# An encoder layer: modulation, projections, convolution and states as one stage over pairs of tiles, in three-term fp32r products

## The chip, the cores and the metric

The kernel runs on one core of a Trainium2 chip (trn2). The metric is the device time of one launch in microseconds. A core has five engines that the text names: TensorE (PE; PEld are its weight loads), VectorE (DVE), ScalarE (ACT), GpSimd (POOL) and SyncE (SP), which here only issues DMAs. Each engine works through its own queue in order and waits on semaphores that others raise.

## What is computed

One encoder layer for two requests, a prompt of 512 tokens and a sample of 1024, both 1024 wide: twelve tiles of 128 tokens, tiles 0 to 3 the prompt's, 4 to 11 the sample's. Cut to what matters here:

```python
mod = silu(c) @ w_ada + b_ada                       # (6 * 1024) per request
sh1, sc1, g1, sh2, sc2, g2 = split(mod)
h = rmsnorm(x, norm1_w) * (1 + sc1) + sh1
proj = h @ w_in                                     # 1024 x 1696
cq, ckv, kr, z, xbc, dt_raw = split(proj)           # 256, 128, 32, 512, 768, 16
y_attn = mla(cq, ckv, kr, ...)                      # 8 heads, over the whole request
xbc = silu(dwconv(xbc, conv_w, 5 taps, centred) + conv_b)
dt = softplus(dt_raw + dt_bias)
# states of each chunk of 128 tokens, forward and backward:
states = einsum(bm, exp(cs[-1] - cs) * dt, x);  carry = carry * exp(cs[-1]) + states
y_ssd = rms((y_fwd + y_bwd + d_skip * x) * silu(z)) * ssd_norm_w
x = x + g1 * (concat(y_attn, y_ssd) @ w_out)
h = rmsnorm(x, norm2_w) * (1 + sc2) + sh2
y = rmsnorm(x + g2 * expert_choice_moe(h))          # 16 experts
```

All inputs and outputs are fp32.

## The kernel before

The kernel is a list of stages, each a block in which the engines have queues of their own, with a barrier between blocks: `modulation`, `projections`, `convolution`, `states`, `attend` (for the prompt and then the sample `keys` and `mixers`), `output`, `choice`, `experts`, `final`. The order of work in a queue is the order in which it is written.

`modulation` takes the first four of twelve slabs of w_ada (512 columns, 2 MB each), through a ring of four buffers: 64 instructions of TensorE a slab with silu(c) as the stationary side (`mod_rows`, L262), a copy by VectorE, one turn into columns (`mod_columns`, L271). SyncE also starts the loads of the first two tiles and of w_in.

`projections` goes over tiles, with the work of the next tile ahead (`tile_pipeline`). ScalarE sums the squares (L407), VectorE scales (L440), TensorE turns eight blocks (L483), both take them with shift and gain (L416, L447), and TensorE multiplies in fp32: latents (L496, 416 columns), z (L500), steps (L514, 16 columns) and xbc by channels, 6 blocks of 128 channels x 128 tokens (L520). An fp32 product is two instructions. Tiles 2 to 9 take one late slab each, between z and the steps (L262 again, and L478 for the turn). All results of all tiles stay in SBUF.

`convolution`: softplus and decays for all tiles at once on VectorE, ScalarE and TensorE, the first tap on ScalarE (L574), the other four on VectorE (L620), 512 or 1024 tokens an instruction. `states` goes over tiles one at a time: silu (L699), turns and B/C products (L753 to L758), weighing of x for both directions (L733), state products (L766), and then `scan` on VectorE over all tiles in both directions (L785, L792). SyncE stores what the mixers need to DRAM, one record of 1920 values a tile.

`mixers` goes over tiles: eight heads of attention, with the SSD products between them. A tile's record and query latents are loaded one or two tiles ahead. The steps `dta`, `dt` and the decays are read from SBUF, where the convolution left them; `terms` on VectorE (L1234) and on POOL (L1061) make the sums' operands out of them.

The experts, which are not changed, already split weights and rows in a high and a low fp32r part and multiply in three terms (L2098 and L2099 for gate and up, L2109 for down).

## Time and profile before

| | us |
|---|---|
| median of 3 runs | 3337.61 |
| lowest, highest | 3326.56, 3339.79 |
| the profiled execution: its time | 3328.14 |
| its span, first to last instruction | 3326.5 |
| modulation, to | 37 |
| projections, to | 378 |
| convolution, to | 431 |
| states, to | 518 |
| keys and mixers of both requests, to | 1162 |

The busy time of an engine is a share of a stage and says nothing by itself of what bounds it: an engine that is never idle bounds; where none is, the waits between them do. The granted clock is a mean of TensorE's two levels, 1.2 and 2.4 GHz, over a stretch: 1.00 is all at 2.4, 0.5 all at 1.2.

### The profile page before, as it was taken

What the parts mean: (1) busy time and instruction counts of PE and PEld (TensorE: products, weight loads), DVE (VectorE), ACT (ScalarE), POOL (GpSimd) and SP (SyncE); (2) the same over time, 40 slices, a digit from 0 to 9 for tenths busy, and PEclk for the clock granted to TensorE, in tenths of its full rate; (3) what the DMA queues carried; (4) which work ended last, traced back from release to release, by engine and by line L of the source; (5) the groups of instructions that cost most, each with busy time, mean ns of one, the idle gap of its engine ahead of it and who ended that gap; (6) DMA issues with size and microseconds to landing.
All of it is one profiled execution on the core that took longest, in us unless ns stands there. A gap on an engine that the chain in (4) does not pass through costs nothing. (4 is left out here: it accounts for less than half of the span.)

```text
span 3326.5 us, 51133 instructions
## 1 busy us (share of the span) xinstructions
PE 2939.6 (88%) x17924; PEld 2396.3 (72%) x17924; DVE 2105.9 (63%) x3908; ACT 1479.8 (44%) x2832; POOL 177.7 (5%) x180
## 2 busy tenths in 40 slices
PE   6999544868999789639999999999999999999993
PEld 4777422544666545339999999999999999999993
DVE  1111474655666523487887788778877887788774
ACT  1111232454445412125555555555555555555553
POOL 0000000101110000000000000000000000000001
PEclk8999766988999989769999999999999999999996
DMA  6121022001011043257777777677767776777764
GB/s 244 64 95 69 19 105 84 31 20 43 21 40 38 21 152 126 76 170 229 247 246 224 238 248 243 225 243 245 240 225 246 246 238 217 254 248 225 231 212 161
DMA packets 355693, 544.53 MB, mean 164 GB/s; under 512 B 11280, under 2 KB 283920, under 8 KB 355600
## 3 DMA queue, kind: packets, MB, share of 16 engines
q1 hardware_dynamic: 346704, 511.83, 45.9%
q0 software_dynamic: 8896, 31.46, 4.0%
q8 instruction: 58, 0.95, 0.1%
q14 instruction: 35, 0.29, 0.0%
HBM read 492.13 MB, written 51.12 MB: 163 GB/s over the span
## 5 line engine op out<-in xcount | busy, mean ns | idle before, releaser
L2098 PE MATMUL banks<-rowsT_parts,weights_high 128*128 128x384 f32 x4096 | 1184.7, 361 | 12.4 <-DVE hidden_parts L2029 7.5
L2099 PE MATMUL banks<-rowsT_parts,weights_low 128*128 128x192 f32 x4096 | 1026.6, 251 | 0.0
L2098 PEld LDWEIGHTS banks<-rowsT_parts,weights_high 128*128 128x128 f32 x4096 | 770.5, 188 | 21.6 <-DVE hidden_parts L2029 9.9
L2099 PEld LDWEIGHTS banks<-rowsT_parts,weights_low 128*128 128x128 f32 x4096 | 783.7, 191 | 1.4
L2109 PE MATMUL banks<-weights_high,hidden_parts 128*128 128x512 f32 x1536 | 435.4, 392 | 0.0
L2016 DVE TENSOR_TENSOR gate_up_sums<-banks,gate_up_sums 128x192 f32<-128x192 f32 x512 | 181.1, 354 | 329.3 <-ACT gate_up_sums L1934 329.3
L1934 ACT ACTIVATE gate_up_sums<-banks 128x192 f32<-128x192 f32 x512 | 164.9, 322 | 453.3 <-PE banks L2099 449.4
L2109 PEld LDWEIGHTS banks<-weights_high,hidden_parts 128*128 128x128 f32 x1536 | 283.4, 188 | 69.9
L2109 PE MATMUL banks<-weights_low,hidden_parts 128*128 128x512 f32 (+1 forms) x1024 | 319.6, 393 | 0.0
L1966 DVE TENSOR_TENSOR weights_low<-slab_up,weights_high 128x1024 fp32r<-128x1024 f32 x256 | 311.6, 1217 | 0.0
L1966 DVE TENSOR_TENSOR weights_low<-slab_down,weights_high 128x1024 fp32r<-128x1024 f32 x256 | 311.2, 1216 | 0.0
L1966 DVE TENSOR_TENSOR weights_low<-slab_gate,weights_high 128x1024 fp32r<-128x1024 f32 x256 | 311.0, 1215 | 0.0
L1908 ACT ACTIVATE weights_high<-slab_up 128x1024 fp32r<-128x1024 f32 x256 | 269.1, 1051 | 0.2 <-DMA slab_up<-w_up 0.2
L1908 ACT ACTIVATE weights_high<-slab_down 128x1024 fp32r<-128x1024 f32 x256 | 264.2, 1051 | 8.5 <-PE banks L2109 7.0
L1908 ACT ACTIVATE weights_high<-slab_gate 128x1024 fp32r<-128x1024 f32 x256 | 267.9, 1047 | 0.0
L2109 PEld LDWEIGHTS banks<-weights_low,hidden_parts 128*128 128x128 f32 (+1 forms) x1024 | 164.9, 161 | 55.6
L1942 ACT ACTIVATE silu_gate<-gate_up_sums 128x192 f32<-128x192 f32 x256 | 92.5, 361 | 226.3 <-DVE gate_up_sums L2016 226.3
L1683 PE MATMUL banks<-arena_modulation 128*128 128x512 f32 x384 | 172.1, 603 | 10.5 <-DMA arena_modulation<-mixed 10.5
L1384 PE MATMUL banks<-arena_modulation 96*128 96x512 f32 x320 | 161.6, 621 | 1.6 <-DVE arena_modulation L1220 1.6
L1225 DVE TENSOR_REDUCE mix_top<-banks 128x1 f32<-128x1024 f32 (+1 forms) x96 | 100.1, 1042 | 75.3 <-PE banks L1384 74.6
L1683 PEld LDWEIGHTS banks<-arena_modulation 128*128 128x128 f32 x384 | 72.3, 193 | 93.7 <-issue 93.7
L1881 POOL DMA_INDIRECT residual<-weighted,rows_out x32 | 49.8, 1557 | 1678.1 <-DVE weighted L2005 1678.1
(263 smaller groups left out, 3389.9 us busy)
## 6 DMA issues: line engine op xcount, KB each, us to landing
slab_gate<-w_gate SPq DMA_DIRECT2D x128, 1024.0 KB, 5.5
slab_up<-w_up SPq DMA_DIRECT2D x128, 1024.0 KB, 7.4
slab_down<-w_down SPq DMA_DIRECT2D x128, 1024.0 KB, 4.9
arena_modulation<-w_ada SPq DMA_DIRECT2D x12, 2048.0 KB, 8.4
arena_modulation<-ssd_tiles SPq DMA_DIRECT2D x12, 960.0 KB, 5.1
arena_modulation<-x_sample SPq DMA_DIRECT2D x16, 512.0 KB, 6.5
mixed<-arena_modulation SPq DMA_DIRECT2D x12, 512.0 KB, 2.8
arena_modulation<-mixed SPq DMA_DIRECT2D x12, 512.0 KB, 5.5
```

The costliest lines, as they stand in the source:

```text
L1225: nc.vector.tensor_reduce(top[:, h % 2:h % 2 + 1], core.banks[:, h % 2 * 1024:h % 2 * 1024 + keys_n], AX_X, ALU.max).then_inc(topped, 1)
L1384: mm = nc.tensor.matmul(core.banks[:, h % 2 * 1024 + k0:h % 2 * 1024 + k0 + 512], qT[j][0:DQK, h, :], kT[0:DQK, h, k0:k0 + 512], start=Tru ...
L1683: mm = nc.tensor.matmul(core.ps[6 * j + half], mt[j][:, k, :], wo[:, k, 512 * half:512 * half + 512], start=(k == 0), stop=(k == 7))
L1881: nc.gpsimd.indirect_dma_start(core.residual, bass.IndirectOffsetOnAxis(ap=rows_out[b][:, 0:1], axis=0), y[b][:], None, compute_op=ALU.add ...
L1908: nc.scalar.activation(like(n, w_hi), unit_of(raw, n), ACT.Copy).then_inc(unit_hi, 1)
L1934: nc.scalar.activation(sums[:, kind, fc % 2], core.ps[2 * (fc % 2) + kind][:, CT:2 * CT], ACT.Copy).then_inc(low_out, 1)
L1942: nc.scalar.activation(sil[:, fc % 2], sums[:, 0, fc % 2], ACT.Silu).then_inc(sil_done, 1)
L1966: nc.vector.tensor_tensor(like(n, w_lo), unit_of(raw, n), like(n, w_hi[:].bitcast(F32)), ALU.subtract).then_inc(unit_lo, 1)
L2016: nc.vector.tensor_tensor(sums[:, kind, fc % 2], core.ps[2 * (fc % 2) + kind][:, 0:CT], sums[:, kind, fc % 2], ALU.add).then_inc(sum_done, 1)
L2098: nc.tensor.matmul(out[:, 0:2 * CT], w_hi[:, u, block], x[:, k, :], start=k == 0, stop=False)
L2099: mm = nc.tensor.matmul(out[:, 0:CT], w_lo[:, u, block], x[:, k, 0:CT], start=False, stop=k == KD - 1)
L2109: mm = nc.tensor.matmul(y_banks[b][0:rows, cols], h_parts[:, fc, tokens], w[:, u, cols], start=step == 0 and first, stop=step == STEPS - 1 ...
```

## The change

`inputs` takes the place of the first four stages. It works on pairs of tiles (`NPAIR` is 6), and its code is written out for all pairs; nothing of it loops.

- Slabs 0 to 3 go through a ring of two buffers. w_in comes in seven pieces, which ScalarE copies to an fp32r high part and VectorE subtracts to a low part; the steps' 16 columns now stand behind the latents', so that one product has 432 columns. The modulated input is split in the same way (`high`, `shift`), from one full-precision buffer (`full`), and turned through one PSUM bank in two halves.
- Each product is three: high x high, high x low, low x high (`terms`). xbc is made for two tiles at once: 256 columns, 6 x 8 x 3 products a pair. Latents and z stay by tile, 24 products each.
- Convolution, softplus, decays, silu, turns, chunk products and states of the pair before run in the same queues, on 256 tokens an instruction. The forward scan keeps one carry (`scan`), the backward one runs at the end of each request (`back`).
- Results go to DRAM by tile: latents (`nat_out`), z (now after silu), steps and decays, x, B/C products, states; the buffers of latents, z and x are single ones.
- `keys` loads latents of all tiles from DRAM before it begins. The mixers read steps and decays from the tile's record, now 1984 values, so `terms` wait for that record.
- The eight late slabs move to the sample's mixers, one a tile, at its last head.

The core of the diff; new functions are cut to what sets the order.

```diff
+            def terms(out, pairs):
+                for k in range(KD):
+                    for n, (a, b) in enumerate(pairs(k)):
+                        mm = nc.tensor.matmul(out, a, b, start=(k == 0 and n == 0), stop=(k == KD - 1 and n == 2))
+                return mm
...
+            def channels(p):
+                for c in range(KC):
+                    xbc(p, c)
+                    if c < 4:
+                        turn(2 * p + 2 + c // 2, c % 2)
+                    if c == 0:
+                        chunk_state(2 * p - 3)
+                    if c == 4:
+                        decays(p - 1)
...
+            for p in range(1, NPAIR):          # TensorE
+                a = 2 * p
+                channels(p)
+                nat(a)
+                zed(a)
+                nat(a + 1)
+                chunk(a - 2)
+                zed(a + 1)
+                chunk(a - 1)
+                chunk_state(a - 2)
...
+            def take_x(t):                     # ScalarE
+                if has(t):
+                    act.wait_ge(xt_mm, t + 1)
+                    if t:
+                        act.wait_ge(xw_done, 2 * t)
+                        act.wait_ge(xn_out, 16 * t)
+                    nc.scalar.activation(xnat, b_S1, ACT.Copy).then_inc(xnat_done, 1)
...
+            for p in range(NPAIR + 1):         # VectorE
+                a, q = 2 * p, p - 1
+                normalise(a + 2)
+                scan(a - 4)
+                weigh(a - 3)
+                soft1(q)
+                if p < NPAIR:
+                    take_xbc(p, 0)
+                soft2(q)
+                shift(a + 2)
+                normalise(a + 3)
+                scan(a - 3)
+                if p < NPAIR:
+                    take_xbc(p, 1)
+                soft3(q)
+                shift(a + 3)
...
+                state_weights(q)
+                if q < NPAIR - 1:
+                    convolve(q)
...
@@ mixers, VectorE
-            def terms(g):
-
+            def terms(g, j):
+
+                dve.wait_ge(tile_in[j], turn_of(g, j) + 16)
                 dve.wait_ge(seg_mm, g * 4)
...
@@ mixers, TensorE
                     if h == 7:
+                        if r:
+                            pe.wait_ge(o_mixed, g)
+                            if before:
+                                late_turn(i - 1)
+                            late_products(i)
                         turn_y(g)
...
-STAGES = [modulation, projections, convolution, states, attend, output, choice, experts, final]
+STAGES = [inputs, attend, output, choice, experts, final]
```

ScalarE's turn of a pair is: table load, `stats` of two tiles, `first_tap`, `soft_exp`, `shift`, `soft_log`, `high`, `shift`, `high`, `decays`, `take_nat`, `take_z`, `silu` of two tiles, `take_nat`, `take_x`, `take_z`, `take_x`.

How the change moves work on VectorE: before, the last rows of the convolution, which stand behind all projections and ahead of all states (L620 the taps, 512 or 1024 tokens each; L626 and L627 the state weights).

```order
L620 SCALAR_TENSOR_TENSOR arena_modulation<-arena_modulation,cols 128x512
L618 REGISTER_ALU
L620 ISA
L620 SCALAR_TENSOR_TENSOR arena_modulation<-arena_modulation,cols 128x1024
L611 REGISTER_ALU
L611 COMPARE_AND_BRANCH
L626 TENSOR_TENSOR arena_modulation<-arena_modulation 128x12x8
L627 TENSOR_TENSOR arena_modulation<-arena_modulation 128x12x8
L632 COPY chunk_decay<-arena_modulation 64x96 x2
```

After, VectorE's rows at the end of pair 5, without tile inputs to shift (L641 the channels of the bank, L648 to L653 the halo, L715 the taps of one pair, L743 the weighing of x):

```order
L641 COPY arena_inputs<-banks 128x2x256
L648 COPY arena_inputs<-arena_inputs 128x6x2
L649 COPY arena_inputs<-arena_inputs 128x6x2
L653 MEMSET arena_inputs 128x6x2
L696 TENSOR_TENSOR arena_inputs<-arena_inputs 128x2x8
L697 TENSOR_TENSOR arena_inputs<-arena_inputs 128x2x8
L700 COPY chunk_decay<-arena_inputs 64x16 x2
L715 SCALAR_TENSOR_TENSOR arena_inputs<-arena_inputs,cols 128x256 x24
```

The taps of a pair now stand between the copies of the next pair's channels and the chunk work, in the queue in which the shifts of the inputs stand too.

SyncE's queue at a middle pair after the change (L378 steps and decays, L369 latents, L373 z, L384 C, L389 x, L391 B/C products). Before, it held in the projections only loads of tiles and slabs.

```order
L378 DMA ssd_tiles<-arena_inputs 128x64
L369 DMA latents<-arena_inputs 128x416
L373 DMA ssd_tiles<-arena_inputs 128x512
L384 DMA ssd_tiles<-arena_inputs 128x128
L378 DMA ssd_tiles<-arena_inputs 128x64
L369 DMA latents<-arena_inputs 128x416
L373 DMA ssd_tiles<-arena_inputs 128x512
L384 DMA ssd_tiles<-arena_inputs 128x128
L389 DMA ssd_tiles<-arena_inputs 128x512
L391 DMA ssd_tiles<-arena_inputs 128x256
L389 DMA ssd_tiles<-arena_inputs 128x512
L391 DMA ssd_tiles<-arena_inputs 128x256
```

The store of x of the tile two back (the first L389) stands behind the stores of z and C of the pair's second tile.

TensorE at the end of a middle tile of the sample's mixers, before (L1397 turns of the probabilities, L1466 the turn of y):

```order
L1384 MATMUL banks<-arena_modulation 128x512 x2
L1393 REGISTER_ALU
L1397 MATMUL banks<-masks,arena_modulation 128x128 x8
L1466 MATMUL banks<-masks,arena_modulation 128x128 x4
L994 REGISTER_ALU
```

and after (L1646 and L1728 are the same two):

```order
L1633 MATMUL banks<-arena_attend 128x512 x2
L1642 REGISTER_ALU
L1646 MATMUL banks<-masks,arena_attend 128x128 x8
L1712 MATMUL banks<-masks,arena_attend 128x128
L1703 ISA
L1706 MATMUL banks<-arena_attend,silu_c_cols 2x128 x32
L1728 MATMUL banks<-masks,arena_attend 128x128 x4
```

One turn and 32 products (64 instructions of the profile) stand ahead of the turn of y.

## Rows read from the trace of the kernel before

**Rows 1.** The page: span; two groups of the experts (busy, mean ns | idle).

```profile
span 3326.5 us, 51133 instructions
...
L2098 PEld LDWEIGHTS banks<-rowsT_parts,weights_high 128*128 128x128 f32 x4096 | 770.5, 188 | 21.6 <-DVE hidden_parts L2029 9.9
...
L1966 DVE TENSOR_TENSOR weights_low<-slab_up,weights_high 128x1024 fp32r<-128x1024 f32 x256 | 311.6, 1217 | 0.0
```

**Rows 2.** Busy time by stretch; columns in the first row.

```profile
core 0: us, PE busy (x) PEld busy (x) DVE busy (x) ACT busy (x) POOL busy (x), PEclk, DMA share, GB/s
...
37.00:378.00 341.00, 331.51 (x2344) 248.91 (x2344) 41.92 (x117) 49.01 (x121) 0.00 (x0) 0.98 0.21 77
378.00:431.00 53.00, 3.57 (x10) 3.06 (x10) 50.60 (x66) 20.06 (x26) 0.00 (x0) 0.51 0.09 30
431.00:518.00 87.00, 38.82 (x204) 23.80 (x204) 57.69 (x164) 28.13 (x85) 0.00 (x0) 0.68 0.32 114
...
546.00:717.00 171.00, 137.74 (x760) 85.10 (x760) 94.00 (x215) 76.02 (x222) 20.73 (x12) 0.88 0.10 36
...
756.00:1162.00 406.00, 360.22 (x2416) 237.85 (x2416) 247.34 (x426) 189.97 (x441) 39.28 (x24) 0.97 0.09 33
```

**Rows 3.** Timeline of TensorE, one tile of the projections (start us, length us).

```profile
270.54 5.75 PE L496 MATMUL banks<-arena_modulation 128*128 128x416 f32 x16
...
283.20 1.93 PE L262 MATMUL banks<-arena_modulation,silu_c_cols 128*2 128x128 f32 x64
...
286.87 10.96 PE L520 MATMUL banks<-arena_modulation 128*128 128x128 f32 x96
297.67 1.04 PE L483 MATMUL banks<-masks,arena_modulation 128*128 128x128 f32 x8
298.54 0.52 PE L496 MATMUL banks<-arena_modulation 128*128 128x416 f32 x1
```

**Rows 4.** Timeline of TensorE in the experts: fp32r products.

```profile
2001.28 1.08 PE L2109 MATMUL banks<-weights_high,hidden_parts 128*128 128x512 f32 x4
...
2003.58 1.08 PE L2109 MATMUL banks<-weights_high,hidden_parts 128*128 128x512 f32 x4
...
2010.16 0.36 PE L2098 MATMUL banks<-rowsT_parts,weights_high 128*128 128x384 f32 x1
2010.36 0.25 PE L2099 MATMUL banks<-rowsT_parts,weights_low 128*128 128x192 f32 x1
2010.45 0.36 PE L2098 MATMUL banks<-rowsT_parts,weights_high 128*128 128x384 f32 x1
```

**Rows 5.** DMA issues of the states (KB each, median us to landing).

```profile
ssd_tiles<-arena_modulation SPq DMA_DIRECT2D x12, 256.0 KB, 2.0
```

**Rows 6.** Groups of VectorE and ScalarE to 518 us (busy, mean ns | idle).

```profile
L620 DVE SCALAR_TENSOR_TENSOR arena_modulation<-arena_modulation,cols x48 | 44.7, 1013 | 0.1
...
L733 DVE TENSOR_TENSOR arena_modulation<-arena_modulation 128x512 f32<-128x512 f32 (+1 forms) x24 | 15.4, 681 | 0.0
...
L440 DVE TENSOR_SCALAR arena_modulation<-arena_modulation,proj_rstd 128x1024 f32<-128x1024 f32 x12 | 9.0, 753 | 0.4
...
L407 ACT ACTIVATE arena_modulation<-arena_modulation 128x1024 f32<-128x1024 f32 x12 | 12.7, 1059 | 190.5 <-DMA arena_modulation<-x_sample 157.5 <-PEq L294 30.7 <-DMA arena_modulation<-x_prompt 2.2
...
L566 ACT ACT_TABLE_LOAD x1 | 1.3, 1283 | 12.2 <-PEq L385 12.2
```

**Rows 7.** Busy time and clock in two stretches of the mixers, columns as in rows 2.

```profile
650.00:700.00 50.00, 43.12 (x274) 28.48 (x270) 29.96 (x68) 21.30 (x62) 4.09 (x3) 0.97 0.03 11
...
550.00:600.00 50.00, 40.61 (x178) 22.96 (x179) 24.38 (x59) 16.10 (x46) 8.22 (x5) 0.77 0.16 60
```

**Rows 8.** Timeline where the keys begin.

```profile
515.66 0.87 DVE L792 TENSOR_TENSOR arena_modulation<-arena_modulation 128x256 f32 x2
...
528.35 0.48 PE L909 MATMUL banks<-masks,arena_modulation 128*128 128x128 f32 x1 [38.78 <-DMA arena_modulation<-w_ukv]
```

**Rows 9.** Timeline where the prompt's mixers begin.

```profile
547.44 2.69 DVE L1234 TENSOR_TENSOR arena_modulation<-masks,arena_modulation 128x1024 f32<-128x1024 f32 x1
...
550.18 0.35 DVE L1209 TENSOR_SCALAR arena_modulation<-arena_modulation,mix_q_rstd 128x256 f32<-128x256 f32 x1
...
552.59 1.90 POOL L1072 TENSOR_TENSOR arena_modulation<-arena_modulation 128x1024 f32<-128x1024 f32 x1 [3.56 <-DMA arena_modulation<-ssd_tiles]
```

More of the change, by code:

```diff
@@ new lines, in shift @@
+            def shift(t):
+                if has(t):
+                    r = request(t)
+                    act.wait_ge(mod_ready, 1)
+                    act.wait_ge(turned, 2 * t + 1)
+                    act.wait_ge(low_done, t)
+                    for k in range(4):
+                        ins = nc.scalar.activation(full[:, k, :], b_T[:, k * P:(k + 1) * P], ACT.Identity,
+                                                   bias=core.mod[:, k, r:r + 1], scale=core.scale1[:, k, r:r + 1])
+                    ins.then_inc(sh_act, 1)
@@ new lines, in take_x @@
+            def take_x(t):
+                if has(t):
+                    act.wait_ge(xt_mm, t + 1)
+                    if t:
+                        act.wait_ge(xw_done, 2 * t)
+                        act.wait_ge(xn_out, 16 * t)
+                    nc.scalar.activation(xnat, b_S1, ACT.Copy).then_inc(xnat_done, 1)
+            act.wait_ge(eps_done, 1)
+            stats(0)
+            stats(1)
+            shift(0)
+            high(0)
+            shift(1)
+            high(1)
+            for i in range(6):
+                weight(i)
@@ new lines, in _ @@
+            stats(2)
+            stats(3)
+            take_nat(0)
+            weight(6)
+            take_z(0)
+            take_nat(1)
+            take_z(1)
+            for t in (2, 3):
+                shift(t)
+                high(t)
+            for p in range(1, NPAIR + 1):
+                a, q = 2 * p, p - 1
+                act.preload_act_table_set("natural_log_exp_and_others")
+                stats(a + 2)
+                stats(a + 3)
+                if q < NPAIR - 1:
+                    first_tap(q)
+                soft_exp(q)
+                shift(a + 2)
+                soft_log(q)
+                high(a + 2)
+                shift(a + 3)
+                high(a + 3)
+                decays(q)
+                if p < NPAIR:
+                    take_nat(a)
+                    take_z(a)
+                silu(a - 2)
+                silu(a - 1)
+                if p == NPAIR - 1:
+                    first_tap(p)
+                if p < NPAIR:
+                    take_nat(a + 1)
+                take_x(a - 2)
+                if p < NPAIR:
+                    take_z(a + 1)
+                take_x(a - 1)
@@ new lines, in by_token, with nat @@
+            def by_token(t, out, cols):
+                high, low = (hT[t // 2 % 2][:, :, part, t % 2 * P:t % 2 * P + P] for part in range(2))
+                return terms(out, lambda k: ((high[:, k, :], w_hi[:, k, cols]), (high[:, k, :], w_lo[:, k, cols]),
+                                             (low[:, k, :], w_hi[:, k, cols])))
+            def nat(t):
+                if t < 2:
+                    pe.wait_ge(high_done, t + 1)
+                    pe.wait_ge(low_done, t + 1)
+                    pe.wait_ge(w_low, 5)
+                if t:
+                    pe.wait_ge(nat_free, t)
+                by_token(t, b_N[:, 0:L_Z], slice(0, L_Z)).then_inc(nat_mm, 1)
@@ new lines, in _ @@
+            rows_to_columns(SLABS - 1)
+            for t in range(2):
+                for half in range(2):
+                    turn(t, half)
+            for t in range(2):
+                nat(t)
+                zed(t)
+            channels(0)
+            for p in range(1, NPAIR):
[8 more added lines that the diff above has]
+                chunk_state(a - 2)
```

1108 lines of the change are left out of this document (625 added, 483 removed).

## The prediction, made before the change was timed

> **What bounds the kernel now.** I read the page first, then one table of busy time by stage, then the timeline where a stage begins or ends. The profiled execution spans 3326.5 us [rows 1]; launch to end it took 3328.1 us, 9.5 us under the median of the runs shown. From 1162 us on nothing is changed, so everything is decided in the first 1162 us [rows 2]. The reader is to see three kinds of stretch there. In the projections (37 to 378) TensorE is busy 331.5 of 341 us at a granted clock of 0.98: it is the bound. In the convolution (378 to 431) VectorE is busy 50.6 of 53 us and TensorE 3.6. In the states (431 to 518) no engine is busy more than 57.7 of 87 us: the engines hand single tiles round, and at the end VectorE scans alone. So 140 us stand in which TensorE does 42 us of work, most of it at a low clock (0.51 and 0.68). In the mixers of the sample (756 to 1162) TensorE is the bound again, 360 of 406 us.
>
> **Projections.** A tile takes 28.0 us, from one L496 to the next (270.54 and 298.54) [rows 3]. The 96 fp32 instructions of L520 run 10.8 us until the transposes of L483 begin, 0.1125 us each, and each brings its own weight load of 128 columns. L262, one late slab, takes 1.93 us.
>
> The change makes every product three fp32r products. The trace has fp32r only in the experts: one pair of 384 and 192 columns takes 0.285 us (2010.16 to 2010.45), and ten products of 512 columns, one after the other, 2.3 us (2001.28 to 2003.58) [rows 4]. For the new products of 256 columns I have two bounds. Each streams for as long as one L520 instruction, which passes 128 columns twice; that gives 0.1125 us. Half of the excess of the experts' pair over a pure stream, added to it, gives 0.127 us. I take 0.115, nearer the row that has the same stream and the same weight load in every instruction. Per pair of tiles the channels then cost 6 x 8 x 3 = 144 x 0.115 = 16.6 us; the two times 24 products of 432 columns, at 0.230 x 432/512 = 0.194, 9.3 us; those of 512 columns 48 x 0.230 = 11.0 us. Transposes, decays, chunk products and states of the pair add 8.5 us (estimate from the L483 rate and the states' 38.8 us for twelve tiles, less its cold part). TensorE's sum is 45.4 us a pair, where projections alone are 56 now.
>
> **The pair's chain.** TensorE will not run unbroken. I follow one pair from the end of the last z product (time 0). ScalarE takes z (0.65); SyncE stores it, then B/C, and only then x of the tile two back, whose buffer is single. That store lands 2.0 us after its issue [rows 5], at about 4.0. ScalarE then copies x (4.6), loads its table (1.28), squares the next input (1.06), and takes the two short steps [rows 6]; VectorE normalises (0.75), at 8.5. TensorE has finished chunk, states and the first 2.8 us of channels at 5.6: it waits 2.9 us for the transposes. The state product behind them waits for scan and weighing on VectorE (1.15 and two of 0.68 us [rows 6]): 2.0 us. Tile two of the pair has the same bank and the same full-precision buffer; its normalising stands behind copy, softplus steps, shift (1.4), ScalarE's high part (1.05) and the low part (1.2) of tile one: 3.3 us more. The convolution of the pair before is 24 operations of 256 elements. 48 of mean 768 take 44.7 us [rows 6], 0.13 us each above a rate of 1.04 ns an element, so 24 x 0.40 = 9.6 us. It ends at 44 us, its silu at 46.8, and TensorE wants it at 47.6: hidden, with 1 us of cover. VectorE works 29 us of the pair and ScalarE 22. A pair with a successor takes 45.4 + 8.2 + 0.7 = 54.3 us; the last one has no transposes and takes 44.
>
> **The stage.** Slabs and first tiles run as now to 37 us. Shifting and splitting two tiles, one after the other, takes 12.5 us. Splitting the weights (13.25 blocks of 1024 elements, 1.22 us each on VectorE [rows 1]) lets the first product begin at 59.5 and takes no more from then on; four token products bring the channels of pair 0 to 82 us. They take 21.2 (two stalls); pair 1 without states 45.3: 148.5. Three pairs of 54.3 and one of 44: 355.5. The tail is serial: convolution of the last pair 12, softplus and decays 10, silu, two chunks and states 14, backward scan 5.1: 41 us. For the clock I add 12 us: TensorE will be busy 84% of a pair; the rows at 81 and 86% have clocks of 0.77 and 0.97 [rows 7], and I go nearer the second. The stage ends at 408.5 instead of 518: **109 us less**.
>
> **What it gives back.** Keys: now 12.7 us pass from the start of VectorE's last addition (515.66) to TensorE's first keys work (528.35) [rows 8]. The latents come from DRAM behind both weights, 1 MB more, and the statistics wait for them: +5 us (0 if the queue is empty, 8 at the states' 114 GB/s). Mixers, twice: VectorE's first terms (L1234, 2.69 us) need no transfer now and the latent is scaled at 550.18; then they wait for the tile, which POOL has at 552.59, and everything in the queue behind them too, the first query's scaling above all: 552.6 + 2.7 - 550.2 = 5 us each [rows 9], +10. The late slabs: 8 x (1.93 + 0.27) = 17.6 us, now in a stage where TensorE bounds too, and about 1.5 at the end, where gains and turn stand ahead of the last norm: +19. In the projections that cost is already in the 109. VectorE's copy and columns (0.5 us a tile) stand in its queue ahead of the masks and lie beside TensorE's slab products. The 2 MB of a slab are asked for one tile (47 us) ahead: nothing. Sum: -109 + 5 + 10 + 19 = -75, so 3253 for this execution and 3263 for the median; I say **3260**.
>
> One rule of the Trainium skill speaks against the change. The rows say: in L520 a weight load and a stream of full height follow each other every 0.1125 us, which is little more than the stream alone [rows 3]. "TensorE: Matmul & The Clock Gate", section "The mechanism", says that a weight load overlaps running products only when the row group differs, and its section on LDWEIGHTS gives 128/1.2, or 107 ns, a load. By that page each product of 256 columns would cost some 0.21 us, and the sum would be an estimated 82 us worse. The trace of fp32 does not agree with it; fp32r with equal widths is not in it.
>
> **Rivals.** (a) No stalls: stores land sooner or the orders fit, TensorE stays at full clock. Three pairs lose 8.3 us each and the 12 us of clock go: 3223. For it: VectorE and ScalarE have 16 us to spare in a pair. (b) The stalls breed a low clock: at 0.8 a fifth of TensorE's rate is missing over 330 us, and what isn't hidden costs 40 us more than I have put: 3300. For it: the row of 0.77 at 81% busy. (c) The weight loads are not hidden. The record gives a load 188 ns [rows 1]; added to each of 864 products of 256 columns that is 162 us: 3420, slower than before. It turns into a loss from 75/864, or 0.087 us, extra on each product. Against it: L520. Near that point it is a draw, 3338. (d) The ring of waits is longer than I see, 68 us a pair or more (a stall at each store of the single buffers, with the clock at half): also a loss, 3350. (e) All as forecast, but slabs stall the sample mixers (VectorE's copy waits for products, the queries for the copy), 5 us a tile: 3300.
>
> **How the numbers follow.** Forecast 0.50; (a) 0.17; (b) 0.15; (e) 0.06; (c) 0.05, of which 0.03 slower; (d) 0.07, half of it within half a per cent of now. The range reaches to (a) and takes in (b) and (e): 3222 to 3305. It also holds the unknown costs: 144 x 6 products between 0.1125 and 0.127 are -2 to +10 us, stalls of 4 to 12 us a pair are -13 to +12. Half a per cent, about what a measurement of this kernel can tell from no change, is 17 us. Faster: 0.50 + 0.17 + 0.15 + 0.06 = 0.88; within: 0.02 + 0.03 = 0.05; slower: 0.03 + 0.04 = 0.07.
>
> **What would show it.** The first keys work should start near 426. A steady pair should take 54 us, products of 256 columns follow at 0.115, and the page should name VectorE's normalising and weighing as what TensorE waited for. A tile of the sample mixers should grow by 2.2 us. The prediction is wrong if the granted clock of the first stage is under 0.9, if VectorE's convolution ends behind the last token product, or if TensorE waits for ScalarE's takes of z and the latents.

## The result, and the profile after

| | before | after |
|---|---|---|
| median | 3332.38 us (4 runs, 3326.56 to 3339.79) | 3251.05 us (4 runs, 3242.06 to 3256.47) |
| profiled execution: span | 3326.5 us | 3251.2 us |

The ratio is 0.975, 95% interval 0.9724 to 0.9776. The forecast was 3260 us, with a range of 3222 to 3305.

Busy time of the last four periods of a pair in the changed kernel; the borders are the starts of TensorE's chunk turns for the first tile of a pair (L929). The columns are as in [rows 2].

```profile
140.60:195.70 55.10, 47.70 (x301) 42.52 (x300) 27.45 (x78) 21.15 (x53) 0.00 (x0) 0.94 0.18 60
195.70:252.40 56.70, 48.98 (x301) 43.54 (x299) 28.39 (x82) 19.40 (x48) 0.00 (x0) 0.91 0.18 59
252.40:310.50 58.10, 50.50 (x301) 45.28 (x301) 27.94 (x81) 22.76 (x59) 0.00 (x0) 0.88 0.14 47
310.50:357.30 46.80, 44.55 (x285) 40.57 (x284) 21.59 (x69) 13.06 (x35) 0.00 (x0) 0.96 0.14 48
```

And the stage as a whole, in head, pairs and tail:

```profile
37.00:78.40 41.40, 23.73 (x104) 20.50 (x105) 21.66 (x27) 22.21 (x31) 0.00 (x0) 0.75 0.42 153
78.40:363.80 285.40, 255.24 (x1620) 232.49 (x1619) 136.91 (x388) 104.43 (x262) 0.00 (x0) 0.93 0.15 52
363.80:404.00 40.20, 14.02 (x70) 9.45 (x68) 27.84 (x96) 9.46 (x25) 0.00 (x0) 0.62 0.18 63
```

These rows answer to those of [rows 2]: TensorE is at work for 89% of the 285 us of the pairs, and of the 140 us in which it had done 42 us of work (378 to 518) a tail of 40 us is left. The places at which TensorE begins something new give an account of the whole. The next rows are its timeline in the changed kernel (start, length; in brackets the idle time before and what ended it). They are the first keys work of the prompt, the first turn of a query, the last turn of the prompt, and the first query and the last turn of the sample, whose first keys work comes at 628.15.

```profile
417.46 0.45 PE L1120 MATMUL banks<-masks,arena_attend 128*128 128x128 f32 x1 [19.57 <-DVE arena_attend L1087]
...
447.18 0.69 PE L1606 MATMUL banks<-masks,arena_attend 128*128 128x128 f32 x2 [12.53 <-DVE arena_attend L1437]
...
619.89 1.12 PE L1672 MATMUL banks<-masks,arena_attend 128*128 128x128 f32 x4 [2.62 <-DVE arena_attend L1525]
...
670.55 0.66 PE L1606 MATMUL banks<-masks,arena_attend 128*128 128x128 f32 x2 [9.98 <-DVE arena_attend L1437]
...
1084.38 1.09 PE L1672 MATMUL banks<-masks,arena_attend 128*128 128x128 f32 x4 [2.68 <-DVE arena_attend L1525]
```

Three of the same places in the kernel before are the first query and the last turn of the prompt and the last turn of the sample. (The first keys work is in [rows 8], the keys of the sample begin at 722.71, its first query at 759.65.)

```profile
550.59 0.69 PE L1357 MATMUL banks<-masks,arena_modulation 128*128 128x128 f32 x2 [4.65 <-DVE arena_modulation L1209]
...
714.48 1.11 PE L1423 MATMUL banks<-masks,arena_modulation 128*128 128x128 f32 x4 [2.62 <-DVE arena_modulation L1296]
...
1156.19 0.66 PE L1423 MATMUL banks<-masks,arena_modulation 128*128 128x128 f32 x4 [2.62 <-DVE arena_modulation L1296]
```

| stretch | before | after | difference |
|---|---|---|---|
| start to first keys work | 528.35 | 417.46 | -110.9 |
| to first query, prompt | 22.24 | 29.72 | +7.5 |
| prompt's mixers | 163.89 | 172.71 | +8.8 |
| to the sample's keys | 8.23 | 8.26 | 0.0 |
| to first query, sample | 36.94 | 42.40 | +5.5 |
| sample's mixers | 396.54 | 413.83 | +17.3 |
| from there to the end | 2170.3 | 2166.8 | -3.5 |

The sum is -75.3 us, the difference of the spans; the forecast was -75.

### The profile page after: what moved, and what is told of

Same layout as the page of the kernel before. It is cut to its first block and busy times, and to the rows that moved or that the text cites. A ratio compares the mean times of both kernels' runs of the same rounds, so it can differ in the third digit from the quotient of the medians.

```text
span 3251.2 us, 50490 instructions
## 1 busy us (share of the span) xinstructions
PE 2884.2 (89%) x17686; PEld 2403.8 (74%) x17686; DVE 2145.1 (66%) x4092; ACT 1527.1 (47%) x2933; POOL 180.9 (6%) x180
## 5 line engine op out<-in xcount | busy, mean ns | idle before, releaser
L1955 PE MATMUL banks<-arena_attend 128*128 128x512 f32 x384 | 170.9, 599 | 9.7 <-DMA arena_attend<-mixed 9.7
L1633 PE MATMUL banks<-arena_attend 96*128 96x512 f32 x320 | 165.2, 633 | 1.6 <-DVE arena_attend L1448 1.6
L1404 ACT ACTIVATE arena_attend<-banks 128x512 f32<-128x512 f32 (+1 forms) x96 | 50.5, 526 | 190.8 <-PE banks L1646 190.8
```

The lines of the kernel that those rows point to most:

```text
L1404: nc.scalar.activation(probT[h % 2][:, 0:half, :], b_pT[:, 0:half * P].rearrange("p (k q) -> p k q", k=half), ACT.Copy).then_inc(pT_act, 1)
L1633: mm = nc.tensor.matmul(core.banks[:, h % 2 * 1024 + k0:h % 2 * 1024 + k0 + 512], qT[j][0:DQK, h, :], kT[0:DQK, h, k0:k0 + 512], start=Tru ...
L1955: mm = nc.tensor.matmul(core.ps[6 * j + half], mt[j][:, k, :], wo[:, k, 512 * half:512 * half + 512], start=(k == 0), stop=(k == 7))
```

## The experiments

All times are medians of four runs. Each ratio is against the kernel before on the same chip, and its 95% interval stands behind it. The kernel before had a median of 3335.57 us on the chip of `e1` to `e4`, 3328.97 on that of `e5` to `e8` and 3327.73 on that of `e9`, so that differences of medians between these groups hold to about 7 us; the ratios and the stretches of the traces don't depend on it. Each kernel has one profiled execution. Unless said otherwise, an edit is made in the changed kernel.

### What the three-term products are worth

`e1_fp32` keeps the joined stage and goes back to one fp32 product; the high parts become fp32 as well.

```diff
-                    for n, (a, b) in enumerate(pairs(k)):
-                        mm = nc.tensor.matmul(out, a, b, start=(k == 0 and n == 0), stop=(k == KD - 1 and n == 2))
+                    a, b = pairs(k)[0]
+                    mm = nc.tensor.matmul(out, a, b, start=(k == 0), stop=(k == KD - 1))
```

> The changed kernel with one fp32 product in place of three fp32r products, everywhere in the first stage. High parts hold the full values, the low parts are still computed (they are zero) and not multiplied, so all work of VectorE and ScalarE stays. Fp32 products at the rate of the projections before (0.719 us for 416 columns): 0.442 us for 256 columns against 3 x 0.1177, 0.747 for 432 against 3 x 0.196, 0.87 for 512 against 3 x 0.232, so 48 x 0.089 + 16 x 0.16 + 16 x 0.175 = 9.6 us a pair. Theory (TensorE bounds the pair, plus stalls of a fixed length): six pairs cost 58 us more, the first keys work moves from 417.5 to about 475, the kernel takes about 3309 us; the join of the stages is then worth about 50 us by itself, the three-term products the other 58. Rival (the ring of waits sets the pair's length, TensorE's rate matters little): under 25 us more, keys before 443, 3275 us.

It took 3292.56 us (0.9869, 0.9845 to 0.9894), 41.5 us more than the changed kernel, and its first keys work came at 463.30, 45.8 us later. That lies between theory and rival, nearer the theory. Timeline of TensorE in a channel block of `e1_fp32` (19 instructions of fp32, two a product), and of the changed kernel (three fp32r products a row pair):

```profile
374.78 4.26 PE L873 MATMUL banks<-h_parts,w_in_high 128*128 128x256 f32 x19
378.88 1.20 PE L918 MATMUL banks<-arena_inputs,masks 128*128 128x32 f32 x10
```

```profile
176.11 0.40 PE L873 MATMUL banks<-h_parts,w_in_high 128*128 128x256 f32 x2
...
176.46 0.40 PE L873 MATMUL banks<-h_parts,w_in_high 128*128 128x256 f32 x2
```

Nineteen instructions in 4.10 us are 0.216 each, 0.432 a product (I had put 0.442); three fp32r products follow in 0.35 us, 0.118 each. With 0.725 against 0.588 for 432 columns and 0.86 against 0.695 for 512 the difference by these rates is 8.6 us a pair, 52 in all, not 58. What TensorE waited for in the pairs (us in total, times, longest), of the changed kernel and of `e1_fp32`:

```profile
PE banks L865 <- DVE arena_inputs L615: 24.8, 8, 3.3
PE banks L948 <- DVE arena_inputs L743: 5.3, 4, 2.2
```

```profile
PE banks L865 <- DVE arena_inputs L615: 20.6, 8, 3.4
PE banks L948 <- DVE arena_inputs L743: 3.1, 3, 1.4
```

The longer products fill 6.4 us of the waits: 52 less 6.4 are nearly the 45.8 of the stage. In the profiled executions the whole grew by 41.8 only: the prompt's mixers took 8.1 us less (see the late slabs, below), and what stands behind the last turn of the sample, which is unchanged, 4.9 more. `e9_fp32_norm`, further down, makes the same edit where the stalls are gone.

### Does TensorE or the ring of waits set a pair?

`e2_two_terms` leaves the third product out.

```diff
-                    for n, (a, b) in enumerate(pairs(k)):
+                    for n, (a, b) in enumerate(pairs(k)[:2]):
```

> The changed kernel without the third product of each three (low part of the second operand is left out of the sum; the low parts are still computed). TensorE's work falls by 12.5 us a pair. Theory (TensorE bounds, next is the convolution of the pair before with 2 us of cover, and the two chains behind the transposes keep their length): a pair gains 12.5 - 0.9 - 0.9 - 3.0 = 7.6 to 8.6 us, the first pair 4, the first two tiles 6.8, in all about 51 us: first keys work near 367, 3200 us, and the trace names ScalarE's silu ahead of the B/C turns, with about 3 us a pair. Rival (nothing else is near the bound): 75 us less, 3176. Rival (a ring of waits sets the pair): under 20 us less.

It took 3216.52 us (0.9643, 0.962 to 0.9666), first keys work at 380.89: 34.5 and 36.6 us less, where 51 were expected. The waits are those expected. TensorE's timeline of one pair, at the chunk's turns and at the first of the two waits for transposes (the second, at 206.56, is 4.29 us):

```profile
178.55 1.12 PE L929 MATMUL banks<-masks,arena_inputs 128*128 128x128 f32 x4 [2.86 <-ACT arena_inputs L544]
...
193.05 1.12 PE L865 MATMUL banks<-masks,arena_inputs 128*128 128x128 f32 x4 [4.13 <-DVE arena_inputs L615]
```

The silu costs 2.86 us (3 expected) and the transposes 0.9 more each. So the chains keep their length when TensorE's work shrinks, as the theory says, and the convolution with its silu is next. What the forecast of this run left out is the clock:

```profile
178.50:231.90 53.40, 38.83 (x220) 34.06 (x220) 29.01 (x84) 21.02 (x55) 0.00 (x0) 0.82 0.20 64
```

0.82 where the same pair of the changed kernel has 0.91. The pair gains 3.3 us instead of 7.6. A gain of TensorE's own work is given back twice here: of 12.5 us of work left out, 6.8 come back as idle time and about 2.3 as longer products. The last pair, without transposes, took 36.8 instead of 46.8 us.

### The first stall: the statistics behind the store of x

The chain as predicted, in the changed kernel (ScalarE, VectorE and SyncE's queue). It starts with ScalarE's take of z; the store of x is issued at 148.84, and ScalarE takes the next x (L554) when it has landed. The table load (L577, 1.28 us) and the statistics stand between that and VectorE's normalising (L615).

```profile
147.36 0.60 ACT L500 ACTIVATE arena_inputs<-banks 128x512 f32<-128x512 f32 x1 [5.49 <-PE banks L873]
...
148.84 0.44 SPq L389 DMA_DIRECT2D ssd_tiles<-arena_inputs  x1
...
151.09 0.60 ACT L554 ACTIVATE arena_inputs<-banks 128x512 f32<-128x512 f32 x1 [3.13 <-DMA ssd_tiles<-arena_inputs]
...
154.74 0.75 DVE L615 TENSOR_SCALAR arena_inputs<-arena_inputs,in_rstd 128x1024 f32<-128x1024 f32 x1 [5.77 <-ACT in_rstd L457]
```

And the three waits of TensorE that follow, 3.21, 0.85 and 3.33 us:

```profile
155.55 1.12 PE L865 MATMUL banks<-masks,arena_inputs 128*128 128x128 f32 x4 [3.21 <-DVE arena_inputs L615]
157.52 1.97 PE L948 MATMUL banks<-arena_inputs 128*64 128x256 f32 x8 [0.85 <-DVE arena_inputs L743]
...
170.22 0.66 PE L865 MATMUL banks<-masks,arena_inputs 128*128 128x128 f32 x4 [3.33 <-DVE arena_inputs L615]
```

`e3_stats_early` moves the statistics of the next pair (`stats`) forward in ScalarE's queue, to right behind the decays of the pair before.

```diff
                 act.preload_act_table_set("natural_log_exp_and_others")
-                stats(a + 2)
-                stats(a + 3)
+                if p == 1:
+                    stats(a + 2)
+                    stats(a + 3)
...
                 decays(q)
+                stats(a + 4)
+                stats(a + 5)
```

> The changed kernel with the statistics of the next pair's two inputs on ScalarE right behind the decays, ahead of the takes of latents, z and x, where they stood behind the take of x that waits for the store of the tile two back. Theory (the first stall of a pair, 3.2 us, and the wait for the weighing behind it, 1.0, both come from that order): both go in the three middle pairs, 12.7 us, and with them about 2 us a pair of products at the low clock: first keys work near 400, 3233 us. The second stall of 3.3 us stays. Rival (the store of x itself holds the pair, through the take of x and the weighing): the stall moves to the state products, under 5 us less. Rival (statistics in the new place push back latents and silu): no gain or a loss.

It took 3225.42 us (0.967, 0.9647 to 0.9693), 25.6 us less; first keys work came at 397.38, 20.1 sooner (17.5 expected). Most of the rest is the prompt's mixers, 168.5 us instead of 172.7. The theory holds: middle pairs take 50.2, 48.8 and 50.2 us. TensorE's waits for the transposes fell from 24.8 us in eight waits to 14.9 in five: what is left is one stall in each of pairs 0 to 4, 1.9 us in pair 0 and 3.2 to 3.3 in the others.

### The second stall: an order, or the single bank?

`e5_stats_norm` is `e3_stats_early`, and VectorE also normalises the second tile of the next pair ahead of its other work.

```diff
                 normalise(a + 2)
+                normalise(a + 3)
                 scan(a - 4)
...
                 shift(a + 2)
-                normalise(a + 3)
                 scan(a - 3)
```

> As e3_stats_early, and VectorE normalises both inputs of the next pair at the head of the pair's queue, where the second stood behind shift and split of the first. Theory (the second stall, 3.3 us a pair in pairs 1 to 4, is only that order): the second turn then waits for the bank alone, 0.3 us; 4 x 3 = 12 us, and the low clock behind each of these stalls, 2 us each: first keys work near 378 against 397.4, 3206 us against 3225. Rival (the bank and the one full-precision buffer hold the second tile back by themselves): the stall stays over 2 us, under 5 us less.

It took 3208.68 us (0.9635, 0.9619 to 0.9651), 16.7 less than `e3_stats_early`, or about 12 by the ratios, since the two ran on different chips; first keys work came at 381.74 (378 expected), 15.6 sooner. Rows of `e5_stats_norm`, the periods of three middle pairs and its waits in all pairs:

```profile
135.30:181.60 46.30, 45.29 (x301) 40.81 (x300) 27.45 (x78) 21.15 (x53) 0.00 (x0) 1.00 0.21 71
181.60:228.10 46.50, 45.47 (x301) 40.67 (x299) 28.43 (x83) 19.43 (x48) 0.00 (x0) 1.00 0.22 72
228.10:274.50 46.40, 45.35 (x301) 40.91 (x301) 27.93 (x81) 19.67 (x51) 0.00 (x0) 1.00 0.17 59
```

```profile
PE banks L951 <- DVE arena_inputs L746: 3.5, 4, 2.6
PE banks L868 <- ACT arena_inputs L466: 1.9, 4, 0.5
PE banks L868 <- DVE arena_inputs L625: 1.1, 4, 0.4
```

TensorE's busy time is 45.3 to 45.5 us a pair: the sum of the prediction, 45.4. The same 301 instructions took 47.7 to 50.5 in the changed kernel. The clock is 1.00 instead of 0.88 to 0.94, and a transpose waits 0.5 us at most: bank and full-precision buffer held nothing back beyond that. A pair gains 8.8, 10.2 and 11.7 us. Idle time falls from 7.4 to 7.7 us a pair to 1.0, which is 6.4 to 6.7 of it; the other 2.4, 3.5 and 5.2 are the same instructions at the higher clock.

### The products again, without stalls

`e9_fp32_norm` makes the edits of `e5_stats_norm` and of `e1_fp32` together.

> e5_stats_norm and e1_fp32 together: no stalls ahead of the transposes, and one fp32 product in place of three fp32r products. By the rates in the traces of e1_fp32 and the changed kernel a pair has 48 x (0.432 - 0.353) + 16 x (0.725 - 0.588) + 16 x (0.86 - 0.695) = 8.6 us more of TensorE's work. Theory (e1_fp32 showed only 41.5 us of 52 because longer products fill stalls and keep the clock up; where TensorE is never idle all of it counts): 6 x 8.6 = 52 us above e5_stats_norm, 3260 us, a middle pair takes 55 us at a clock of 1.00. Rival (the products' rates overstate the difference, the sum is 41.5 wherever it stands): 3250 us.

It took 3257.36 us (0.9785, 0.976 to 0.9809), 48.7 more than `e5_stats_norm`, or 50 by the ratios; first keys work came at 421.85, 40.1 later. One of its pairs:

```profile
200.00:254.00 54.00, 54.00 (x223) 36.27 (x222) 29.36 (x86) 21.24 (x54) 0.00 (x0) 1.00 0.19 63
```

TensorE is never idle in this window, the clock is 1.00, and the L929 of three pairs stand at 201.75, 255.09 and 308.67: 53.3 and 53.6 us, 7.0 above `e5_stats_norm`, not 8.6. Theory and rival both missed the reason: `e5_stats_norm` still had idle time to fill. Its stretches from the first product to the last pair:

```profile
56.00:95.00 39.00, 36.52 (x220) 33.89 (x221) 15.92 (x24) 15.25 (x26) 0.00 (x0) 0.93 0.31 111
95.00:135.30 40.30, 39.44 (x281) 37.59 (x280) 23.83 (x66) 23.00 (x57) 0.00 (x0) 1.00 0.16 54
...
274.50:321.70 47.20, 44.58 (x285) 40.58 (x284) 21.60 (x69) 13.07 (x35) 0.00 (x0) 0.96 0.14 47
```

With the three pairs above that is 2.5 + 0.9 + 3.1 + 2.6 = 9.1 us of idle time, 9 of the missing 12. The other 3 lie in the work itself: by TensorE's busy time a middle pair has 53.3 us of work against 45.4, 7.9 more and not 8.6, so the rival had a part of it. The profiled executions differ by 45.3 us, 5.2 more than the stage: 2.3 between the first keys work and the prompt's first query, 2.7 behind the last turn of the sample. The mixers have no part in it (164.6 and 164.5 us for the prompt). The rest of the 48.7 is between median and profiled execution. So in this stage the three-term products are worth 40 to 46 us, and the join of the stages the larger rest of the 110.9: `e1_fp32`, which has the join alone, begins the keys 65 us sooner than the kernel before.

### What a late slab costs in the sample's mixers

`e6_slab_eighth` makes 4 of the 32 products of each late slab and leaves the others out.

```diff
-                for k in range(KD):
+                for k in range(1):
```

> The changed kernel with one eighth of each late slab's products in the sample's mixers (4 of 32; the other rows of the slab are left out of the sum). Loads, copies and turns stay. Theory (TensorE bounds there, a slab costs its products): 8 x 1.69 = 13.5 us less between the first query's turn and the last turn of the sample, 413.8 to 400.3, 3238 us. Rival (the growth of 17.3 us is the wait of the queries for VectorE's copy of the slab's rows, or the transfer of 2 MB a tile): under 4 us less. Rival (VectorE and ScalarE take over as the bound once the products are gone): 5 to 9 us less.

It took 3234.82 us (0.9714, 0.9698 to 0.9731). Busy time of the sample's mixers in the changed kernel and in `e6_slab_eighth`:

```profile
670.00:1085.00 415.00, 378.20 (x2935) 251.97 (x2936) 245.29 (x441) 187.41 (x432) 38.32 (x24) 0.97 0.18 66
```

```profile
660.00:1062.00 402.00, 364.66 (x2487) 239.70 (x2488) 244.81 (x441) 187.27 (x432) 37.96 (x23) 0.98 0.19 68
```

TensorE does 13.5 us less, and the stretch from the first query to the last turn (660.22 to 1061.49) is 12.6 us shorter. The theory holds to 1 us, and no wait on VectorE's copy is among TensorE's. This pair of executions also answers for the prompt's mixers, whose code is the same in both, over windows of one length:

```profile
435.00:612.00 177.00, 141.80 (x730) 87.27 (x730) 92.41 (x211) 72.08 (x208) 21.51 (x12) 0.83 0.09 33
```

```profile
435.00:612.00 177.00, 138.71 (x760) 85.78 (x760) 93.95 (x215) 76.11 (x222) 21.50 (x12) 0.87 0.10 36
```

In the second, 30 more instructions are done in the same time at 0.87. From first query to last turn, executions with the same code there took 172.7 us (the changed kernel), 164.6 (`e1_fp32`), 172.6 (`e2_two_terms`), 168.5 (`e3_stats_early`), 164.5 (`e5_stats_norm`), 164.7 (here) and 164.6 (`e9_fp32_norm`); before it was 163.9. TensorE's idle time in them is 27 us each time; what differs is its busy time, 147 us at a clock of 0.84 in the changed kernel and 138 at 0.88 here. So the +8.8 of the account is the clock of one execution and not a cost of the change. What sets the clock of an execution is not shown.

### The prologues

```diff
             def first():                     # mixers, VectorE
-                terms(lo, 0)
                 for step in range(7):
                     front(step, lo, 0, 0)
+                terms(lo, 0)
...
+                sp.wait_ge(sem("nat_out"), 16 * NT)          # keys, SyncE
+                sp.dma_start(nat, core.nat.rearrange("t p c -> p t c")[:, :, QL:NAT]).then_inc(sem("kv_in"), 16)
+                sp.dma_start(wukv, io["w_ukv"][0]).then_inc(sem("w_qkv_in"), 16)
                 sp.dma_start(wuq, io["w_uq"][0].rearrange("(k p) n -> p k n", p=P)).then_inc(sem("w_qkv_in"), 16)
-                sp.dma_start(wukv, io["w_ukv"][0]).then_inc(sem("w_qkv_in"), 16)
-                sp.wait_ge(sem("nat_out"), 16 * NT)
-                sp.dma_start(nat, core.nat.rearrange("t p c -> p t c")[:, :, QL:NAT]).then_inc(sem("kv_in"), 16)
```

> The changed kernel with VectorE's first terms of each request behind the seven steps of the first query, and the latents of the keys loaded ahead of the two weights. Theory (both prologues grew since the query's scaling stood behind the wait for the tile's record): the first turn of the queries comes at 440.6 instead of 447.2 and 5.8 us sooner in the sample, of which the terms give back 1 to 2 each, and the keys begin 2 us sooner: 11 us less, 3240 us. Rival (the record is needed right after, so the wait only moves to the first state-space product): under 4 us less.

It took 3240.98 us (0.9711, 0.9684 to 0.9737), 10 less. Its interval overlaps that of the changed kernel, so the trace has to decide. In the changed kernel the prompt's first query is scaled (L1437) behind the terms (L1463), and beside GpSimd's own (L1291); both engines wait for the tile's record, whose load SyncE issues at 436.42:

```profile
436.42 0.42 SPq L1247 DMA_DIRECT2D arena_attend<-ssd_tiles  x1
...
444.00 1.23 DVE L1463 TENSOR_TENSOR arena_attend<-masks,arena_attend 128x1024 f32<-128x1024 f32 x1 [7.86 <-DMA arena_attend<-ssd_tiles]
444.33 2.65 POOL L1291 TENSOR_TENSOR arena_attend<-masks,arena_attend 128x1024 f32<-128x1024 f32 x1 [443.74 <-DMA arena_attend<-ssd_tiles]
445.14 1.99 DVE L1437 TENSOR_SCALAR arena_attend<-arena_attend,mix_q_rstd 128x256 f32<-128x256 f32 x1
```

The forecast of the prologue had 5 us; this one took 7.5. The scaling beside GpSimd takes 1.99 us instead of 0.35, but the terms ahead of it take 1.23 instead of 2.69 [rows 9], and from the start of the first to the end of the second VectorE needs 3.1 us in both kernels. (The 2.69 stood beside GpSimd's L1061, from 547.15 to 549.04.) The other 2.4 us are the load of the tile's record: VectorE has it 7.6 us after its issue here, and GpSimd had it 5.1 us after its issue before the change (at 547.46). In `e6_slab_eighth`, whose code is the same up to there, it came 5.1 us after its issue, and from the first keys work to the first query it took 27.4 us, 5.2 above the kernel before:

```profile
436.74 0.42 SPq L1247 DMA_DIRECT2D arena_attend<-ssd_tiles  x1
...
441.85 1.23 DVE L1463 TENSOR_TENSOR arena_attend<-masks,arena_attend 128x1024 f32<-128x1024 f32 x1 [5.39 <-DMA arena_attend<-ssd_tiles]
```

In `e4_prologue` (the scaling of the prompt's first query on VectorE, and the turn of the sample's on TensorE):

```profile
445.62 0.35 DVE L1437 TENSOR_SCALAR arena_attend<-arena_attend,mix_q_rstd 128x256 f32<-128x256 f32 x1 [3.96 <-ACT mix_q_rstd L1325]
...
664.67 0.66 PE L1606 MATMUL banks<-masks,arena_attend 128*128 128x128 f32 x2 [4.75 <-DVE arena_attend L1437]
```

TensorE's wait before the queries falls from 12.53 to 5.86 us and from 9.98 to 4.75. From the sample's keys to its first query the stretch is 37.17 us, as before the change (36.94) and 5.2 less than after it; from first query to last turn it is 412.66 against 413.83, so in the sample the wait doesn't come back. In the prompt that stays open: the three executions that have this edit (`e4_prologue`, `e7_all`, `e8_all_tail`) took 173.2, 169.9 and 171.4 us from first query to last turn, at clocks of 0.81 to 0.84, and four of the seven without it took 164.5 to 164.7. The order of the loads gave less: from the last tile's L929 to the first keys work 25.70 us instead of 27.37, and now TensorE waits for w_uq. In the whole, first keys work came at 422.58, 5.1 us later, in code that the edit doesn't touch: the first product began 2.5 us later, and the three middle pairs took 3.9 more, at a clock of 0.88 in each.

### All together, and the tail

`e7_all` is `e5_stats_norm` with `e4_prologue`. `e8_all_tail` also splits the last convolution:

```diff
                 take_cb(a - 1)
                 if p == NPAIR - 1:
-                    convolve(p)
+                    convolve(p, 1, 3)          # taps 1 and 2
...
                 soft2(q)
+                if p == NPAIR:
+                    convolve(q, 3, 4)
...
+                if p == NPAIR:
+                    convolve(q, 4, 5)
                 state_weights(q)
```

> e5_stats_norm and e4_prologue together: the gains lie in different stretches and add up, 3206 - 10 = 3196 us. If they don't add up, the granted clock of the prompt's mixers is what differs, which went from 0.83 to 0.88 between executions of the same code.

> As e7_all, and the last pair's convolution in three parts, with the softplus of the pair between them, where the softplus stood behind the whole convolution. Theory (the tail is one chain: convolution, softplus, decays, a table load, silu): the decays fall beside the convolution and silu begins right behind its last tap, 8 us less than e7_all. Rival (the takes of z and x on ScalarE and the table loads hold the softplus anyway): under 3 us less.

`e7_all` took 3202.37 us (0.9616, 0.96 to 0.9632), `e8_all_tail` 3198.23 (0.9604, 0.9588 to 0.962). The sum of the two gains alone would be 3199 by the medians and about 3195 by the ratios, so some 4 to 7 us are missing. As the expectation allows, the prompt's mixers differ: they took 169.9 us in `e7_all` and 164.5 in `e5_stats_norm`, at clocks of 0.84 and 0.88. First keys work came at 378.15 and, with the tail split, at 375.04, 3 us sooner, 2.5 of them behind the first L929 of the last pair; the rival said under 3, and the intervals of the two overlap. Rows of `e8_all_tail`: ScalarE's table load and its first step of the softplus (L515), and the decays on TensorE.

```profile
330.10 1.28 ACT L577 ACT_TABLE_LOAD   x1
334.79 0.23 ACT L515 ACTIVATE arena_inputs<-arena_inputs 128x32 f32<-128x32 f32 x1 [3.41 <-DVE arena_inputs L664]
...
340.94 2.34 PE L925 MATMUL banks<-arena_inputs,masks 128*128 128x32 f32 x10 [4.48 <-DVE arena_inputs L691]
```

The rival's number came true and its reason did not: ScalarE has taken x and loaded its table at 331.38 and then waits 3.41 us for VectorE. VectorE works without a gap over 0.3 us from 327.1 to 343.3, with taps 1 and 2, scan, weighing, softplus steps, tap 3, scan, the decays' input (L691) and tap 4 one behind the other. The decays come 3.0 us sooner than in `e7_all` (340.94 and 343.96), and silu too (345.19 and 348.21), 1.9 us behind the last tap; but the last tap itself now ends at 343.3 instead of 337.5, since softplus and decays stand ahead of it in the same queue. The theory had left that out. `e8_all_tail` is the fastest measured, 53 us under the changed kernel by the medians, 49 by the ratios, and 4% under the kernel before.

## Why the prediction was right, point by point

- **Products.** 0.115 us forecast for 256 columns, 0.118 measured; 0.194 and 0.196 for 432; 0.230 and 0.232 for 512. Rival (c) is out: no weight load shows between the products. The page "TensorE: Matmul & The Clock Gate" of the Trainium skill says in its section "The mechanism" that a weight load overlaps running products only where the row group differs, which with its 107 ns a load gives an estimate of 0.21 us a product; this trace does not agree with it, as L520 did not [rows 3]. (The same section also has loads pulled ahead into a background weight buffer, which would fit.)
- **TensorE's sum of a pair.** 45.4 us forecast, 45.3 to 45.5 busy in `e5_stats_norm`, where nothing disturbs it.
- **The chain of a pair.** Stalls of 2.9, 2.0 and 3.3 us forecast; 3.21, 0.85 to 1.18 and 3.33 measured, with the stores, the statistics and the normalising at the places named. `e3_stats_early` and `e5_stats_norm` took them away one by one. The middle one was put too long, by about 1 us.
- **The convolution.** 9.6 us forecast, 9.6 measured; the cover was 2 us, not 1. `e2_two_terms` used it up and showed it.
- **The stage.** First product 59.5 forecast, 56.4 measured; channels of pair 0 from 82 and from 78.4; end of the tokens of pair 1 at 148.5 and at 147; end of the stage 408.5 and 404. The three middle pairs took 169.9 us, against 162.9 forecast without and 175 with the 12 us for the clock. Taken apart with `e5_stats_norm`, they are 136.1 us of work (136.2 forecast), 22.7 of idle time (26.7 forecast) and 11.1 of low clock, with some 3 more of that ahead of them (12 forecast for the stage). So the clock was sized about right, and the waits were put 4 us too long, 3 of them in the middle stall. The tail was 41 us by the forecast and 40 measured.
- **The clock.** I wrote that a clock of the first stage under 0.9 would prove the prediction wrong. It is 0.87 from 37 to 404 (285.4 us at 0.93 between a head at 0.75 and a tail at 0.62). By that sign the prediction would be wrong, and its time was right all the same. The sign was badly made: head and tail wait for VectorE and ScalarE (TensorE is busy 57% and 35% there), so their clock should cost little, though no run separates that. In the pairs it was 0.93. Rival (b) was true in kind: the stalls cost clock, 2.4 to 5.2 us a pair, not the 13 more that its 40 us would need.
- **Keys.** +5 forecast. From the end of VectorE's last scan to the first keys work 11.8 us passed before and 13.65 after (403.81 to 417.46): +1.8. In both, weights have to land first.
- **Prologues.** +5 each forecast, +7.5 and +5.5 measured. The cause was as forecast, the scaling behind the wait for the record, and `e4_prologue` confirmed it. The 2.4 us more in the prompt are the load of the tile's record, which landed late in this execution. The step missed that GpSimd would start with VectorE and slow its scaling to 1.99 us; it put the terms at 2.69 where they took 1.23, and the two errors cancel, which was luck.
- **Late slabs.** 17.6 us in the tiles forecast, 17.3 measured. Rival (e) has no row. The 1.5 us forecast at the end can't be told from the other differences behind the mixers.
- **Not in the sum:** +8.8 in the prompt's mixers and -3.5 behind all of it. The first is the clock of this execution, the second is in code that is unchanged but for the end of the last late slab. Together with 3 us of the prologues they hide that stage and keys came 7 us better than forecast (-110.9 against -104): that the total came out at -75 to the microsecond is luck.
- **Rival (a)** gave 3223 for a stage without stalls, 37 us less than the forecast; `e5_stats_norm` shows 3209. The rival sized the three middle pairs rightly: 138 us by it, 139.2 measured. It counted no other pair, but pairs 0 and 1 have the second stall too, and the keys began at 381.74, 7 us sooner than the 389 that the rival gives (37 less than 426). Most of the rest is the scale: forecast and rival start from a median of 3337.61, and on the chip of `e5_stats_norm` the kernel before had 3328.97.

## What to carry to other kernels

Where one engine is meant to bound and three others hand tiles round it, write each engine's queue out for one period and look for short operations that stand behind a store or behind the previous tile's longer work: three calls moved in two queues brought the end of this stage 36 us forward (38 us by the ratios of the whole), and the single bank and the full-precision buffer, which looked like the limit, were not. A stall of the matrix engine costs its length and mostly some clock behind it: the pairs that stood idle for 7.4 to 7.8 us took 9 to 12 us more than those of `e5_stats_norm`, while of the pairs of `e3_stats_early`, idle for 3.5 us each, one kept a clock of 1.00 and two had 0.97. And compare stretches between executions of the same code before giving a difference of 2 or 3% to an edit.

## What was not expected of the hardware

- Three fp32r products are cheaper than one fp32 product of the same shape: 0.353 against 0.432 us for 256 columns, 0.695 against 0.86 for 512.
- Behind the first stall the next products ran at the low level. Timeline of TensorE of the changed kernel, three products in 0.64 us instead of 0.35:

```profile
160.02 0.41 PE L873 MATMUL banks<-h_parts,w_in_low 128*128 128x256 f32 x1
...
160.66 0.41 PE L873 MATMUL banks<-h_parts,w_in_low 128*128 128x256 f32 x1
```

- The clock of the same code differs between executions: 0.83 and 0.87 over the same window of the prompt's mixers, and 8 us from first query to last turn. The middle pairs of the first stage, with the same code, took 55.1, 56.7 and 58.1 us in the changed kernel and 57.8, 58.2 and 57.8 in `e4_prologue`.
- VectorE's scaling of 256 elements took 1.99 us beside a product of GpSimd (L1291), and 0.35 in `e4_prologue`, where GpSimd began 1.3 us after its end.
- The load of a tile's record before the first query of the prompt landed 7.6 us after its issue in the changed kernel and 5.1 us after it in `e6_slab_eighth`, with the same code up to there.
